# Five RMS norms applied after the matmuls they feed, tokens loaded ahead of the weights, and a router that picks by maximum

## The reference, cut to what matters

```python
h = concat([meta, x])                                            # 272 tokens
h = h + 0.5 * swiglu(rmsnorm(h, ffn1_norm), w_gate, w_up, w_down)    # norm 0, d_ff 2816
u = rmsnorm(h, mix_norm) @ w_in                                      # norm 1
h = h + mixer(u) @ w_out                                             # attention A, sparse attention B
h = h + 0.5 * swiglu(rmsnorm(h, ffn2_norm), w_gate, w_up, w_down)    # norm 2, 256 tokens from here on
for l in range(2):
    u = rms_norm(h, norm1_g[l]) @ w_in_2[l]                          # norm 3 (l=0), norm 5 (l=1)
    h = h + mixer_2(u) @ w_out_2[l]
    t = rms_norm(h, norm2_g[l])
    group = argmax(softmax(t @ w_group + b_group))                   # 1 of 4 groups
    two   = top2(softmax(logits of the 8 experts of that group))     # weights renormalised
    h = h + sum over experts of weight * (silu(t @ w_gate) * (t @ w_up)) @ w_down
out = rms_norm(h, final_g)
```

## Time and profile before

| what | value |
|---|---|
| median of 3 runs | 1349.73 us (1345.92 to 1351.85) |
| profiled execution | 1347.56 us, span 1345.7 us |
| busy in the span | PE 1200.3 us, DVE 423.5, ACT 389.1, POOL 27.5 |
| chain that ended last | PE 72%, DMA 19%, DVE 5% |
| first expert chunk released, layer 0 and 1 | 795.77 us (DMA share 0.04 from 790 to 796), about 1140.4 us |
| one weight chunk split in feed-forward 1 | ACT 1.91 us (L698), then DVE 2.29 us (L1613) |
| DVE two-input product or copy, 128x272 | 0.43 to 0.44 us (L1640, L1697, L1604); 128x544 0.72 us (L1619) |
| DVE reciprocal; ACT root; table load | 1.85 us at 272 tokens, 1.75 at 256; 0.49; 1.28 |
| ACT copy or square 128x272; square 128x1088 | 0.40 to 0.43; 1.11 |
| one pair of gate and up chunks on PE | 12.11 us at 272 tokens (44.87 to 56.98), 11.36 at 256 (472.60 to 483.96) |
| one projection unit on PE | 3.45 us (249.71 to 253.17) |

### The profile page before, as it was taken

The page is one execution under the profiler, slowest core; times in us unless marked ns, Lnnn a source line. Parts: engine busy times, 40 slices in busy tenths (PEclk is TensorE's granted clock), DMA queues, the critical chain, the costliest instruction groups (busy, mean ns, idle before and its releaser), DMA issues.

```text
span 1345.7 us, 18094 instructions
## 1 busy us (share of the span) xinstructions
PE 1200.3 (89%) x7656; PEld 905.0 (67%) x7656; DVE 423.5 (31%) x849; ACT 389.1 (29%) x744; POOL 27.5 (2%) x44
## 2 busy tenths in 40 slices
PE   5999999999999799999999969877779996997775
PEld 3999999777567699999886845532248675542221
DVE  4444444250352544455336131100022623111001
ACT  4333433122252444434237121100013532111001
POOL 0000000100000000000100000000002000000000
PEclk8999999899968899999999989988879998998887
DMA  9444544523101355545265359999985824999996
GB/s 382 164 179 167 184 161 157 199 107 124 64 1 52 137 188 188 188 160 187 92 258 242 116 229 423 424 422 422 424 350 218 333 92 173 423 422 423 423 423 269
DMA packets 45334, 322.68 MB, mean 240 GB/s; under 512 B 5192, under 2 KB 5448, under 8 KB 7104
## 3 DMA queue, kind: packets, MB, share of 16 engines
q1 hardware_dynamic: 43728, 314.18, 59.4%
q0 software_dynamic: 688, 3.69, 0.8%
q10 hardware_dynamic: 832, 3.57, 0.7%
HBM read 320.36 MB, written 3.16 MB: 240 GB/s over the span
## 4 chain that ended last, share of the span: by engine, by line
PE 72%; DMA 19%; DVE 5%; issue 1%; ACT 1%; SPq 1%; ACTq 0%; DVEq 0%
PE bank L1082 11%; DMA arena<-in_stream 10%; PE bank L1039 10%; PE bank L1041 10%; PE bank L1040 10%; DMA ring<-in_stream 8%; PE bank L1049 6%; PE bank L1499 3%; PE bank L1478 3%; PE bank L1518 2%; PE bank L1116 2%; PE bank L1092 2%; PE bank L1002 1%; PE bank L1212 1%; PE bank L1329 1%
## 5 line engine op out<-in xcount | busy, mean ns | idle before, releaser
L1039 PE MATMUL bank<-r_hi,w_hi 128*128 128x272 f32 (+1 forms) x1056 | 303.1, 287 | 17.1 <-DVE r_lo L1619 13.9
L1041 PE MATMUL bank<-r_hi,w_lo 128*128 128x272 f32 (+1 forms) x1056 | 302.8, 287 | 0.0
L1040 PE MATMUL bank<-r_lo,w_hi 128*128 128x272 f32 (+1 forms) x1056 | 302.5, 286 | 0.0
L1039 PEld LDWEIGHTS bank<-r_hi,w_hi 128*128 128x128 f32 x1056 | 201.1, 190 | 18.4 <-issue 18.3
L1613 DVE TENSOR_TENSOR w_lo<-ring,w_hi 128x2048 fp32r<-128x2048 f32 x66 | 151.3, 2292 | 176.4 <-ACT w_hi L698 176.4
L1041 PEld LDWEIGHTS bank<-r_hi,w_lo 128*128 128x128 f32 x1056 | 201.1, 190 | 0.0
L1040 PEld LDWEIGHTS bank<-r_lo,w_hi 128*128 128x128 f32 x1056 | 200.7, 190 | 0.0
L698 ACT ACTIVATE w_hi<-ring 128x2048 fp32r<-128x2048 f32 x66 | 126.1, 1912 | 142.7 <-PE bank L1041 138.5
L1082 PE MATMUL bank<-xn,ring 128*128 128x256 f32 (+1 forms) x624 | 146.5, 396 | 8.1 <-DVE xn L1604 8.1
L1082 PEld LDWEIGHTS bank<-xn,ring 128*128 128x128 f32 x624 | 121.9, 197 | 31.0 <-issue 10.5
L1948 DVE TENSOR_TENSOR arena<-arena,bank 128x256 f32<-128x256 f32 x16 | 6.7, 421 | 243.5 <-ACT arena L939 243.5
(11 more groups left out here) (305 smaller groups left out, 1286.9 us busy)
## 6 DMA issues: line engine op xcount, KB each, us to landing
ring<-in_stream SPq DMA_DIRECT2D x160, 1024.0 KB, 5.0
arena<-in_stream SPq DMA_DIRECT2D x68, 1024.0 KB, 26.0
sm<-in_stream SPq DMA_DIRECT2D x18, 1024.0 KB, 26.4
G<-in_stream SPq DMA_DIRECT2D x10, 1024.0 KB, 23.3
w_ukv<-in_stream SPq DMA_DIRECT2D x10, 1024.0 KB, 24.6
sq<-in_stream SPq DMA_DIRECT2D x10, 1024.0 KB, 26.6
xn<-in_stream SPq DMA_DIRECT2D x10, 1024.0 KB, 26.2
mixT<-in_stream SPq DMA_DIRECT2D x8, 1024.0 KB, 26.6
```

Source lines behind the costliest of these rows:

```text
L1039: mm(dst, hi, r_hi[:, k, 0:T], start=first, stop=False)
L1040: mm(dst, hi, r_lo[:, k, 0:T], start=False, stop=False)
L1041: return mm(dst, lo, r_hi[:, k, 0:T], start=False, stop=last)
```

## The change

The diff does five things.

1. **Feed-forwards.** ACT and DVE split `hT` times the gain (not `xn`) into `r_hi` and `r_lo`, tile by tile (`first_high`, `second_high`, `low`). PE starts the gate matmuls without waiting for the norm. DVE adds the squares of the eight tiles (`sum_squares`), PE sums over features with one matmul (`late_norm`, behind the first pair of chunks), and the factor is multiplied onto the gate bank (into `sil`) and onto the up bank (into `hid`) before silu and the product: three DVE operations for each hidden tile where there was one.
2. **Mixers.** ACT writes `hT` times the gain into `hg1` or `hg2`. The first four units (`gained_unit`) read that; `late_norm` stands behind the second of them; DVE saves their banks times the factor (`scale_unit`, in place of ACT's saves). Later units read `xn` as before.
3. **Chunks of weights** 0 and 1 of feed-forward 2 are split before the residual of the mixer.
4. **Tokens.** SP issues both large token tiles before the first weight chunk; the second of them was on ACT's queue. `xtok` moves in `arena`.
5. **Router.** The logits outside the group get a large negative number; `max` and `match_replace` mark the two best of 32; `comb` comes from an exponential of all 32 values, masked. `places_psum` is raised after two matmuls, and again after two more.

The core of the diff ("..." marks what is left out):

```diff
-        xtok = carve("xtok", 4 * CH, 3, D)
+        xtok = carve("xtok", FR, 3, D)
+        hg1 = carve("hg1", AR - KT * T1, KT, T1)
+        hg2 = carve("hg2", AR - 2 * CH, KT, T2)
...
-            sp.dma_start(xtok[:, 0, :], x_tok[0:128]).then_inc(S("x_loaded"), 16)
+            for t in range(2):
+                sp.dma_start(xtok[:, t, :], x_tok[128 * t:128 * t + 128]).then_inc(S("x_loaded"), 16)
...
-            act.dma_start(xtok[:, 1, :], x_tok[128:256]).then_inc(S("x_loaded"), 16)
...
+            def first_high(d):
+
+                if d < 4:
+                    act.wait_ge(S("input_saved"), d + 1)
+                    src = hT[:, d, :]
+                else:
+                    act.wait_ge(S("xT_ready"), d + 1)
+                    src = bank[d][:, 0:T1]
+                    copy(hT[:, d, :], src, ACT.Copy).then_inc(S("high_saved"), 1)
+                copy(r_hi[:, d, :], src, ACT.Copy, scale=gain(G_NORM + d)).then_inc(S("x_hi_ready"), 1)
...
+                split_w(f, 2)
+                split_w(f, 3)
+                token_root(2 * f)
+                split_w(f, 4)
+                silu(0)
+                silu(1)
+                for c in range(1, FC):
+                    if c > 1:
+                        split_w(f, 2 * c + 2)
+                    silu(2 * c)
+                    silu(2 * c + 1)
...
+            def late_norm(n):
                 off, T = span[n]
...
+                pe.wait_ge(S("squares_summed"), NTH[n] + 1)
+                mm(bank[4 if n in GAINED_AT else 7][:, 0:T], ones, sq[:, 0, 0:T], start=True, stop=True).then_inc(S("sumsq_ready"), 1)
...
+                            if i == 3 and j == 1:
+                                pe.wait_ge(S("root_ready"), FFN_ROOT[f])
...
+            def gained_unit(u, base, at, c0, n, l):
...
+                    if u == base:
+                        pe.wait_ge(S("gained_ready"), KT * GAINED_AT[n] + max(k, l) + 1)
...
+            def sum_squares(n):
+                T = span[n][1]
+                dve.wait_ge(S("squares_ready"), 2 * NTH[n] + 2)
+                for w in (4, 2, 1):
+                    ins = V.tensor_tensor(sq[:, 0:w, 0:T], sq[:, 0:w, 0:T], sq[:, w:2 * w, 0:T], ALU.add)
...
             def norm(n):
...
+                scale_unit(0)
+                scale_unit(1)
                 for k in range(KT):
                     V.scalar_tensor_tensor(xn[:, k, 0:T], hT[:, k, off:off + T], gain(G_NORM + KT * n + k), rstd[:, 0, 0:T],
                                            ALU.mult, ALU.mult).then_inc(S("xn_ready"), 1)
...
+                scale_unit(2)
+                scale_unit(3)
...
+                for c in range(FC):
+                    scale_gate(2 * c)
+                    scale_gate(2 * c + 1)
+                    if c > 1:
+                        split_w(f, 2 * c + 2)
+                    scale_up(2 * c)
+                    scale_up(2 * c + 1)
+                    if c == 0:
+                        split_w(f, 4)
+                    product(2 * c)
+                    product(2 * c + 1)
...
+                for t in range(2):
+                    ins = V.max(e8[:, t, :], t48[:, t, :])
...
+                    ins = V.match_replace(comb[:, t, :], two[:, t, :], t48[:, t, :], TAKEN)
...
+                V.tensor_scalar(sel[:, :, :], comb[:, :, :], 0.5 * TAKEN, None, ALU.is_lt).then_inc(S("sel_ready"), 1)
...
-                dve.wait_ge(S("places_psum"), l + 1)
+                dve.wait_ge(S("places_psum"), 2 * l + 1)
```

More of the change, by code:

```diff
@@ L698, in split_w @@
                 copy(w_hi[:, q % 2, :], chunk((A_FFN1, A_FFN2)[f] + q), ACT.Copy).then_inc(S("w_hi_ready"), 1)
-            def split_x(f):
-                for j in range(4):
-                    act.wait_ge(S("xn_ready"), KT * 2 * f + 2 * j + 2)
-                    copy(r_hi[:, 2 * j:2 * j + 2, 0:FW[f]], xn[:, 2 * j:2 * j + 2, 0:FW[f]], ACT.Copy
-                         ).then_inc(S("x_hi_ready"), 1)
             def split_hid(f, c):
@@ L776, in save_o @@
                     copy(u["out"], src, ACT.Copy).then_inc(S("o_saved"), 1)
+            act.wait_ge(S("gains_scaled"), 1)
+            first_high(0)
+            first_high(1)
+            split_w(0, 0)
+            for d in range(2, KT):
+                first_high(d)
+            split_w(0, 1)
+            act.wait_ge(S("high_saved"), 4)
             squares(0)
@@ L795, in save_latent @@
                 copy(ql_sq[:, t, 0:T2], bank[4 + t % 2][:, 0:T2], ACT.Square).then_inc(S("qlat_saved"), 1)
-            for t in range(4):
-                save(t, lambda: copy(uT[:, 14 + t, NMETA:T1], bank[t % 4][:, 0:T2], ACT.Copy))
             save(4, lambda: copy(ikT[:, :], bank[0][:, 0:T1], ACT.Copy))
@@ L842, in _ @@
             steps(SEG_1, (save_T, 2), (save_o, 3), (exps, 0), (save_last, 0), (subln_root, 3))
+            split_w(1, 0)
+            split_w(1, 1)
+            for d in range(KT):
+                second_high(d)
             squares(2)
@@ L851, in v @@
                     return bank[u % 4][:, 0:T2]
-                act.wait_ge(S("pad_ready"), l + 1)
-                for t in range(2):
-                    save(u0 + t, lambda: copy(upad[:, t, 16:272], v(t), ACT.Copy))
-                for t in range(2):
-                    save(u0 + 2 + t, lambda: copy(qbT[:, t, :], v(2 + t), ACT.Copy))
                 for t in range(2):
@@ L917, in _ @@
                 act.wait_ge(S("router_parts"), 4 * l + 4)
-                copy(small[:, 44:46], small[:, 40:42], ACT.Exp).then_inc(S("router_exps"), 1)
+                copy(t48[:, :, :], t48[:, :, :], ACT.Exp).then_inc(S("router_exps"), 1)
                 def x_gain(k):
@@ L1125, in _ @@
                 ins.then_inc(S("xT_ready"), 1)
-            norm(0)
             ffn(0, A_FFN1, 0)
-            norm(1)
-            pe.wait_ge(S("rb_loaded"), 32)
-            mm(bank[7][0:8, :], rb[:, :], bcst[:, C_OH:C_OH + ROW], start=True, stop=True).then_inc(S("bias_psum"), 1)
             def dots(n):
@@ L1657, in residual @@
                                            ).then_inc(S("residual_ready"), 1)
+                    if k == 1 and d > 0:
+                        low(1, d - 1)
+                if k == 1:
+                    low(1, KT - 1)
             def maxes(g):
@@ L1693, in weights, with save_input @@
                 dve.wait_ge(S("probs_ready"), g + 1)
-            for d in range(KT):
+            dve.wait_ge(S("gains_loaded"), 16)
+            V.tensor_scalar(gn[:, 0:64], gn[:, 0:64], math.sqrt(D), None, ALU.mult).then_inc(S("gains_scaled"), 1)
+            def save_input(d):
                 dve.wait_ge(S("xT_ready"), d + 1)
                 V.tensor_copy(hT[:, d, :], bank[d][:, 0:T1]).then_inc(S("input_saved"), 1)
-            dve.wait_ge(S("gains_loaded"), 16)
-            link(V.tensor_scalar(gn[:, 0:64], gn[:, 0:64], math.sqrt(D), None, ALU.mult))
-            norm(0)
+            save_input(0)
+            save_input(1)
+            dve.wait_ge(S("gains_scaled"), 1)
+            dve.wait_ge(S("input_saved"), 2)
+            low(0, 0)
+            low(0, 1)
+            save_input(2)
+            save_input(3)
+            split_w(0, 0)
+            dve.wait_ge(S("input_saved"), 4)
+            for d in range(2, KT):
+                low(0, d)
+            split_w(0, 1)
             ffn(0)
@@ L1829, in _ @@
                 V.reciprocal(tok_rstd, tok_root).then_inc(S("router_parts"), 1)
+                two = small[:, 48:64].rearrange("p (t a) -> p t a", t=2)
+                link(V.memset(small[:, 48:64], -TAKEN))
                 dve.wait_ge(S("router_parts"), 4 * l + 2)
@@ L1899, in _ @@
-                ins.then_inc(S("comb_ready"), 1)
+                for t in range(2):
+                    ins = V.tensor_tensor_reduce(comb[:, t, :], t48[:, t, :], sel[:, t, :], 1.0, 0.0, ALU.mult, ALU.add,
+                                                 den[:, t:t + 1])
+                    if t == 1:
+                        link(ins)
+                w1 = small[:, 116:118]
+                link(V.tensor_tensor(den, den, psel, ALU.mult))
+                link(V.reciprocal(w1, den))
+                V.tensor_tensor(comb[:, :, :], comb[:, :, :], bc(w1, NE), ALU.mult).then_inc(S("comb_ready"), 1)
@@ L1955, in _ @@
                 make_slots(0)
-                link(V.tensor_reduce(load[:, :], bank[1][:, 2 * NE:3 * NE], AX_X, ALU.max))
+                dve.wait_ge(S("places_psum"), 2 * l + 2)
+                link(V.tensor_reduce(load[:, :], bank[0][:, 0:NE], AX_X, ALU.max))
                 V.tensor_copy(load_i[:, :], load[:, :]).then_inc(S("load_known"), 1)
```

243 lines of the change are left out of this document (127 added, 116 removed).

## The result

The changed kernel took 1310.94 us in the median of 4 runs (1310.44 to 1316.09); the kernel before 1348.65 us in 4 runs. The ratio is 0.9728, with a 95% interval of 0.9695 to 0.9761: it is faster by 2.7%. The forecast was 1299; 12 us of the gain that it expected are missing. Profiled execution against profiled execution it is 1310.77 against 1347.56, a gain of 36.8 where the sum said 49.0.

What follows compares the result with a forecast made beforehand. PE was taken to bound most stages, DMA of expert chunks the last part of each layer. Terms summed to -49.0 from 1347.6, giving 1298.6, stated as 1299; own range 1294 to 1305, wide range 1291 to 1311.

Steps and rivals of the forecast that it cites:

- rival 4: Feed-forwards: DVE becomes the bound, a product waiting for silu ahead of a weight split; 1321, chance 8%; 1350 or more, 3%.
- Mixer 1: At mixer 1's norm PE goes on after the last down matmul without the gap; -7.3 us.
- Feed-forward 2: At feed-forward 2's start PE begins without waiting for split activations, first pair done at 459.8 instead of 472.60; -12.8 us.
- Layer 0: At layer 0's mixer norm PE starts its units right behind the last down matmul; -8.4 us.
- Layer 1: At layer 1's mixer PE waits for weight chunk 0, landing 10.0 us after issue; -0.7 us, bounds +1.5 to -9.
- the cover inside the feed-forwards: Within feed-forward pairs, DVE's added products fit beside the weight splits; cost 0, slack 1.3 us.
- The down starts: Where down matmuls start in each feed-forward, PE's wait grows from 1.66 to 2.4 us; +0.8 us, twice.
- The routers: In each layer's router, shorter selection on DVE and two place matmuls instead of five; -3.5 us each, -7.1 in all.
- DVE beside POOL: In the pooling mixers, POOL's sums stretch DVE's `xn` products; +0.5 us in each layer, +1.0 in all.
- the start: From launch to the second pair of feed-forward 1: earlier tokens and late norm; -15.3 us, bounds -11 to -17.5.
- so I take 7.7: At the start the gains land at 7.7 us instead of 12.95, and DVE's first instruction waits for them.
- rival 3: At the start the gains land as late as before, at 12.95; +5 us, 1304, chance 6%.

Runs made afterwards that it cites:

- before_again: The kernel before, unchanged, run once more for a second trace; 1353.36 us in its one run.
- experiment 7: Changed kernel with the old choice of experts put back (two searches on DVE, five matmuls for the places); 1317.44 us, ratio 0.9773.
- pool_late: Changed kernel with GpSimd's sums of the pooling mixer waiting until all eight normed tiles are written; 1313.42 us in 2 runs.
- experiment 9: Both kernels run once more, unchanged, for second traces: the kernel before 1353.36 us, the changed kernel 1310.43 us.
- experiments 3: Changed kernel, with DVE forming one hidden product before the last up scaling in each feed-forward's last pair; 1312.03 us, ratio 0.9713.
- gains_first: Changed kernel with the gains moved from ACT's queue to SP's, behind the token tiles and ahead of the weight chunks; 1304.85 us, ratio 0.9664.
- gains_table: Changed kernel with gains loaded ahead of the weights on SP's queue and ACT's table load ahead of its wait; 1304.73 us, ratio 0.9669.
- experiment 5, pe_pad: Changed kernel with 64 already met waits put in PE's program behind its transposes; 1305.60 us, ratio 0.9700.
- small_late: Changed kernel with layer 1's 1.8 MB transfer on ACT's queue issued later, behind ACT's squares and root; 1304.32 us, ratio 0.9651.
- best_down: Changed kernel with gains_table, small_late, pool_late, 64 met waits before layer 0's selection, and an earlier hidden product at down starts; 1297.41 us, ratio 0.9621.

## Why the prediction was right and where it was wrong

The measured 1310.94 lies outside the forecast's own range of 1294 to 1305. That the wide range ends at 1311 is no merit: its upper part was made for rival 4, which did not come.

**Right.** The mechanism held at each norm: PE goes on without a gap, and what is gained shows as a shift between fixed points. Mixer 1: -7.3 from the last down matmul to its 8 wide ones, forecast -7.3. That the two agree to a tenth is in part luck: the stretch took 26.5 us in the trace of before, with the clock down behind the gap as the step had it, but 25.0 in before_again, where it was not. Feed-forward 2: -12.4 from the output projection to its last down matmul, forecast -12.0 with its down start. Layer 0: -7.6, forecast -8.4 + 0.5. Layer 1: the chunk binds, as the step named it, and landed 9.8 us after issue where 10.0 was said. The pairs stayed at 12.11, so the cover inside the feed-forwards is as worked out, and rival 4 did not come. The down starts wait 1.9 instead of 1.66, less than the 2.4 of the step. The routers gave 5.0 and 4.3 (experiment 7) where 3.5 each stood: up to the gathers it is 3.9 in each layer, and what follows closed up too. DVE beside POOL: the term took 7.2 us for the eight products, with each stretched to one POOL sum, and 7.17 were measured; it cost 0.57, forecast 0.5. The Trainium skill's rule ("SBUF — State Buffer", Who interferes with whom), by which the two block each other whole, has the direction: alone the products took 3.25. A full block in turn would have taken 3.25 plus the seven sums that ran in that time, 6.2 as they stand there and 5.7 in pool_late, so 8.9 to 9.4; the measured 7.17 is less.

**Wrong, first step: the gains in the start, "so I take 7.7".** They landed at 10.87. The step inferred from packet sizes how two queues share the engines; no row showed it. On ACT's queue, behind two other transfers and beside 1 MB of tokens and then the chunks on SP's, they needed 9.2 us, and on SP's queue ahead of the chunks 5.7. This is rival 3 at about three fifths of its size, and had 6%. It made 3.0 of the 3.8 us missing there. Of the rest 0.5 is a longer half-speed stretch (5.6 us, not 4.6), and 0.3 a slip of the sum: the 44.87 that it subtracts from is the start of ACT's split, 0.3 behind PE's own start of the second pair (44.61), while its 29.6 is PE's. Experiment 1 shows the first part: with the gains early the first gate matmul stands at 14.73 where 14.9 was said.

**Wrong, second step: between "Mixer 1" and "Feed-forward 2" the sum has no term, and "+0.8 twice" has none for the clock.** The prediction took half-speed stretches away where a gap closed, and looked for no new ones. The first down start cost 1.5 us more by the clock, where its wait was 0.5 less than said. Mixer 1 behind its norm gave back 4.7 us: 1.9 between the 8 wide and the 16 wide matmuls, 2.9 in the attention. From the down start to the output projection PE was busy at the lower level for 37 us in the trace of before and for 52 in the one of after (summed over windows of 1 us). Half of the difference, 7, would overstate the cost, since in the attention the lower clock also fills PE's waits (experiment 9); by the fixed points it is 6.3. Nor did the clock gain elsewhere what the sum had counted on: its mean over the whole program is 0.939 and 0.936 in the two traces of before, 0.942 and 0.934 in the two of the changed kernel.

What it is not: not the length of the wait alone (experiments 3 and 9), and not the late norm alone, since gains_first and gains_table have it and kept the full clock at the down start and at the 8 wide matmuls. In the attention it is no property of the change: 2.8 us is only that the trace of before had it short. At the 8 wide matmuls the case is open: against before_again 3.3 us would be missing there, not 1.9. And the missing gain is not one trace's bad luck, for the medians too are only 37.7 us apart, where 49.0 were forecast.

**Not in the sum at all: 2 us behind the branch of layer 0** (experiment 5), the row L1543 <- issue: from the gathers to the freed chunk 11.2 us, in before 9.2, in pe_pad 8.9. Against it stands what the routers gave beyond their terms, 0.4 in layer 0 and 0.9 in layer 1. The expert phase of layer 0 took 1.6 us longer, from the freed chunk to the scatter 196.0 us where before had 194.3; small_late had 194.4 and best_down 194.6 with the same instructions there, so this too is spread between executions.

Point by point the missing 12.3 are then: start 3.8, down start 1.0, mixer 1 0.1 + 4.7, feed-forward 2 and layer 0's norm -0.2, router 0 with its stall 1.6, experts 1.6, layer 1's start 0.7, router 1 -0.7, last experts -0.3.

**What stays open:** what decides where the clock falls in a stretch of short matmuls, and whether the change has a part in the stretch at the 8 wide ones. Each execution had it a little different, and no edit tried here set it.

## What to carry to other kernels

Behind an edit that moves everything, a sum from one trace is no better than the spread of PE's clock between executions; give the range that width, and compare fixed points before a wait is blamed. When a norm or a root leaves the critical path, the next in line is what it needs first: here 0.2 MB of gains that had always had time. A weight chunk that PE now waits for wants its queue and its neighbours looked at: moving one transfer that nobody needs for 30 us was worth as much as half of the norms' gain in a feed-forward.

## What the runs showed that was not expected

- 64 waits that are met already, in PE's program, took away a stall of 1.5 us some 730 us later; the stall ends 1.2 to 1.5 us behind a 16 KB block of instructions in all eight traces that have it.
- The eight products and POOL's sums overlap in part (7.17 us for 3.25 and 5.7 to 6.2 us of work), neither freely nor in turn.
- The 237 matmuls of mixer 1's attention took 52.2 to 64.7 us, with no edit near them.
- At the start the matmuls run at half the rate, 11 in 2 us against 18, while the clock column prints 1.00; the trace has no clock record there, so the matmuls have to be counted.
